# Indexer scores of two heads in one insertion between the projection units of a two-layer decoder

## The chip, the cores and the metric

The kernel runs on one core of a Trainium2 chip. The metric is the device time in microseconds of one execution, from the first to the last instruction; lower is better. Five engines work side by side, each through its own list of instructions in order: TensorE (PE, with its weight loads shown apart as PEld), VectorE (DVE), ScalarE (ACT), GpSimd (POOL) and SyncE (SP, which here only issues loads). They meet in semaphores.

## The reference, cut to what matters

Two decoder layers on 256 tokens of width 2048. A layer has one combined projection, three token mixers (sparse attention, a convolution, cross-attention into 256 memory tokens), a gated merge, and an MLP. The part that the change touches is the indexer of the sparse attention:

```python
# 16 indexer heads of width 64; iq (tokens, 16, 64), ik (tokens, 64), iw (tokens, 16)
s_idx = jnp.einsum('bqhd,bsd->bqhs', iqb, ik).astype(jnp.float32)
index = jnp.einsum('bqh,bqhs->bqs', iwb.astype(jnp.float32), jax.nn.relu(s_idx)) * idx_scale
causal = key_pos[None, :] <= q_pos[:, None]
index = jnp.where(causal[None], index, -jnp.inf)
sel_val, sel_idx = lax.top_k(index, topk)      # topk = 64 of 256 keys
```

Tokens are handled in two tiles of 128. A query of the first tile may only see keys 0 to 127, so its scores with keys 128 to 255 are masked whatever they are.

## The kernel before, in words

Nearly all the work is projection. Each 512-column block of a weight matrix is a group of 8 units; a unit (L535 to L548) holds 256 rows of the matrix. SP loads the weights in chunks of 1 MB, two units each. ACT copies a unit to a rounded high part `hi` (L805), DVE subtracts to get the low part `lo` (L1075), and PE multiplies: 12 matmuls of 128x128 by 512 columns (L545 to L547), accumulated in one of two PSUM buffers. `hi` and `lo` have four slots, so ACT may fill unit n once PE has finished unit n - 4, and PE can be up to four units behind what DVE delivers.

Everything else is written into this stream by hand. A front of 11 groups (88 units, n = 0 to 87) and the first 32 units of the merge are unrolled, and a function `side(n)` on each engine says what follows unit n there. ACT, DVE and POOL do at unit n + 4 what belongs to PE's insertion after unit n (`EMPTY_AFTER = 4`). All waits are semaphores; no planner is involved.

The indexer scores are such insertions. After unit n = 36 + s, for s = 0 to 15, PE computes head s (`scores`, L598 to L601): for each of the two query tiles one float32 matmul of 64 rows against all 256 keys, into bank `s % 2` of the PSUM tile `sc`. The trace shows each float32 matmul as two weight loads and two matmuls, so a head has four of each. Even heads lie in partitions 0 to 63 of `iqT` and `ikT`, odd heads in 64 to 127 (`ik_twice` holds the keys twice). At its step 40 + s ACT takes the ReLU of the bank (L913, 128x512), and at the same step DVE adds it to `index` with the head's weight, one instruction for each query tile (L1216, L1218). At its step 55 POOL masks the 256 keys of both tiles (L1531).

Around this lie: fills (L558: four transposes of 128 columns) after units 38 to 41, 45 and 46; from DVE step 51 one convolution tap per step, from step 56 two or three (L1136), from step 58 on every third step a round of the top-k search (L1149, L1154); at ACT's step 52 and DVE's and POOL's step 53 the norm of the memory keys (L929, L931, L1257, L1518 to L1523). From n = 79 on the attention heads are inserted, with full 128-row score matmuls through the same line 601.

DVE works through its list in order. What it does for the index at a step stands ahead of the split of the next unit.

Of the kernel before, what the change touches and what calls it, by code (L numbers as in the profile page):

```python
# [93 lines left out]
INDEX_AT = 36  # L94
# [38 lines left out]
def fills_until(name):  # L133
# [24 lines left out]
              "tp_hi": 78, "score": 28, "sc0": 15, "sc1": 14, "squared": 24, "x_new": 20,  # L158
              "dve_step": 153, "pool_step": 106, "gain_in": 48, "mem_in": 32, "front_in": 16 * FRONT_DMAS,
              "ln_in": 32, "bias_in": 32 * CB, "parked": 32, "x_back": 16, "mean_ready": 3, "rstd_ready": 3,  # L160
              "scaled": 10, "ik_here": 2, "ikwT_here": 1, "ik_turned": 1, "iq_turned": 2,
              "relu_used": IDX_HEADS, "causal_done": 2, "chosen": 1,
# [65 lines left out]
def build(nc, x, mem, positions, norm1_g, w_in, q_norm_g, k_norm_g, mem_norm_g, w_mem_kv, mq_norm_g,  # L228
# [3 lines left out]
    with ctx:  # L232
# [4 lines left out]
        def at(name, shape, offset, dt=F32):  # L237
            n = 4
            for s in shape[1:]:
                n *= s  # L240
            assert base + offset + n <= nc.sbuf_usable_end, name
            return nc.alloc_sbuf_tensor_at(name, shape, dt, offset=base + int(offset))
# [50 lines left out]
        relu = at("relu", [P, 2, T, SEQ], S + 22 * kb)  # L293
        index = at("index", [P, T, SEQ], S + 26 * kb)
# [64 lines left out]
        sc = ctx.enter_context(nc.psum_tensor("sc", [P, 2, T, SEQ], F32))  # L359

# [166 lines left out]
        def _(pe):  # L527
# [70 lines left out]
            def scores(bank, pairs):  # L598
                pe.wait_ge(sc_free[bank], here.next(f"sc{bank}"))
                for t, (a, b) in enumerate(pairs):  # L600
                    mm = pe.matmul(sc[:, bank, t, :], a, b, start=(t == 0), stop=(t == T - 1),  # L601
                                   skip_group_check=True)
                mm.then_inc(sc_full, 1)

            def head_output(j):

                emptied(("p", j, 0))
                b = here.fill(("o", j, 0))
                pe.wait_ge(tp_free[b], here.now(f"tp{b}"))
                o = tp[:, b, 0:2, :].rearrange("p a d -> p (a d)")  # L610
                for kt in range(T):
                    if j < MEM_HEADS:
                        v = mv_tok[:, kt, j]
                    else:
                        v = kv_tok[:, kt, KV_HEADS + (j - MEM_HEADS) // (HEADS // KV_HEADS)]
                    pT = mem_pT if j < MEM_HEADS else attn_pT
                    mm = pe.matmul(o, v, pT[:, j % 2, kt, :], start=(kt == 0), stop=(kt == T - 1))  # L617
                mm.then_inc(tp_full, 1)

            def side(n):  # L620
# [55 lines left out]
                if INDEX_AT <= n < INDEX_AT + IDX_HEADS:  # L676
                    j, a = divmod(n - INDEX_AT, 2)
                    if n == INDEX_AT:
                        emptied(("ik", 0, 0), ("iq", 1, 1))
                    half = slice(a * IDX_DIM, (a + 1) * IDX_DIM)  # L680
                    scores(a, [(iqT[half, j, t * P:(t + 1) * P], ikT[half, :]) for t in range(T)])
# [108 lines left out]
        def _(act):  # L790
# [50 lines left out]
            def side(n):  # L841
# [66 lines left out]
                s = n - INDEX_AT - EMPTY_AFTER  # L908
                if s in range(IDX_HEADS):
                    act.wait_ge(sc_full, here.next("score"))  # L910
                    if s >= 2:
                        act.wait_ge(relu_used, here.next("relu_used"))
                    act.activation(relu[:, s % 2], sc[:, s % 2], ACT.Relu).then_inc(sc_free[s % 2], 1)  # L913
                    if s == IDX_HEADS - 1:
                        here.next("relu_used", 2)
# [137 lines left out]
        def _(dve):  # L1053
# [123 lines left out]
            def side(n):  # L1177
# [28 lines left out]
                if n - INDEX_AT - EMPTY_AFTER in range(IDX_HEADS):  # L1206
                    s = n - INDEX_AT - EMPTY_AFTER
                    if s == 0:
                        here.next("sc0")
                        dve.wait_ge(ik_turned, here.next("ik_turned"))  # L1210
                    here.next(f"sc{s % 2}")
                    dve.wait_ge(sc_free[s % 2], here.now(f"sc{s % 2}") + 1)
                    for t in range(T):
                        w = iw[:, t, s:s + 1]
                        if s == 0:
                            ins = dve.tensor_scalar(index[:, t], relu[:, 0, t], w, None, ALU.mult)  # L1216
                        else:
                            ins = dve.scalar_tensor_tensor(index[:, t], relu[:, s % 2, t], w, index[:, t],  # L1218
                                                           ALU.mult, ALU.add)
                    ins.then_inc(relu_used, 1)  # L1220
                    dve.wait_ge(relu_used, here.next("relu_used"))
                    here.next("score")
# [220 lines left out]
        def _(pool):  # L1443
# [30 lines left out]
            def side(n, l):  # L1474
# [53 lines left out]
                if n == INDEX_AT + EMPTY_AFTER + IDX_HEADS - 1:  # L1528
                    pool.wait_ge(relu_used, here.next("relu_used", IDX_HEADS))
                    alone()  # L1530
                    pool.affine_select(out=index[:, :, :], in_=index[:, :, :], pattern=[[P, T], [-1, SEQ]],  # L1531
                                       compare_op=ALU.is_ge, fill=UNSEEN, base=0,
                                       channel_multiplier=1).then_inc(causal_done, 1)
# [128 lines left out]
```

## Time and profile before

| | us |
|---|---|
| median of 3 executions (lowest, highest) | 2988.55 (2987.88, 2988.84) |
| profiled execution, its span (no other time of it is given) | 2989.6 |
| PE busy | 2917.6 (98%) |
| PE weight loads busy | 2389.9 (80%) |
| DVE busy | 1748.7 (58%) |
| ACT busy | 1355.1 (45%) |
| POOL busy | 318.0 (11%) |
| DMA, mean | 187 GB/s |
| indexer score matmuls, 128 in the trace | 402 ns each on average |

The span counts from the first to the last instruction of the profiled execution, 1.05 us more than the median, which is under 0.04%. Matmuls are pipelined: the next starts while the last one's result drains, so the distance between two starts is what a matmul costs, and the busy time of one is longer. In the timeline a row is: start, duration, engine, line, operation, output and inputs, rows*columns of the array, shapes, and how many instructions were merged into it; brackets hold the idle time before it and what ended it. For each layer the indexer scores lie in one stretch, about 115 to 180 us and 1599 to 1664 us from the span's start.

### The profile page before, as it was taken

How to read it: one execution, taken by the hardware profiler on the slowest of the kernel's cores; microseconds unless marked ns; L12 is line 12 of the kernel's file. 1: busy time of each engine (PE TensorE's matmuls, PEld its weight loads, DVE VectorE, ACT ScalarE, POOL GpSimd, SP SyncE). 2: the span in 40 equal slices, each digit the busy share in tenths (PEclk: the TensorE clock that was granted, in tenths of full speed). 3: DMA queues.
4: the chain of work that ended last, by engine and by line, in shares of the span. 5: the costliest groups of instructions: out<-in, count | busy, mean ns of one | idle time of the engine just before them, and what ended most of it. 6: DMA issues, size and time to landing. Idle time of an engine off the chain costs nothing.

```text
span 2989.6 us, 38386 instructions
## 1 busy us (share of the span) xinstructions
PE 2917.6 (98%) x13120; PEld 2389.9 (80%) x13120; DVE 1748.7 (58%) x1849; ACT 1355.1 (45%) x1673; POOL 318.0 (11%) x329
## 2 busy tenths in 40 slices
PE   7998899999999999999999989999999999999998
PEld 6776788888888888888877767888888888888887
DVE  4689655556555555555545896555565545555554
ACT  5443654444443444434445436444444434344443
POOL 1158300000000000000020682000000000000000
PEclk9999999999999999999999999999999999999999
DMA  7544456565655656555564444666556565565653
GB/s 270 187 162 131 151 170 210 192 228 197 203 185 191 191 188 188 189 188 190 186 220 169 149 141 145 183 208 225 197 200 202 188 190 190 186 192 185 196 184 127
DMA packets 274090, 558.65 MB, mean 187 GB/s; under 512 B 13168, under 2 KB 13168, under 8 KB 271376
## 3 DMA queue, kind: packets, MB, share of 16 engines
q1 hardware_dynamic: 266384, 523.53, 53.1%
q0 software_dynamic: 5888, 30.02, 3.4%
q10 hardware_dynamic: 1664, 3.15, 0.3%
q8 instruction: 84, 1.38, 0.2%
q14 instruction: 70, 0.57, 0.1%
HBM read 550.37 MB, written 6.29 MB: 186 GB/s over the span
## 4 chain that ended last, share of the span: by engine, by line
PE 88%; DVE 6%; issue 4%; ACT 1%; DMA 1%; DVEq 0%; POOL 0%; ACTq 0%; POOLq 0%
PE acc L545 28%; PE acc L547 28%; PE acc L546 28%; DVE conv_acc L1136 3%; PE tp L558 3%; PE sc L601 1%; DVE lo L1075 1%; ACT hi L805 1%; PE tp L617 1%; DMA conv_bias<-in_conv_o_b 1%; DVE index L1154 0%; DVE index L1218 0%; DMA pos_i<-in_positions 0%; DVE head_sum L1257 0%; DVE s_buf L1166 0%
## 5 line engine op out<-in xcount | busy, mean ns | idle before, releaser
L1075 DVE TENSOR_TENSOR lo<-raw,hi 128x1024 fp32r<-128x1024 f32 (+1 forms) x1008 | 1237.6, 1230 | 1191.9 <-ACT hi L805 1182.9
L805 ACT ACTIVATE hi<-raw 128x1024 fp32r<-128x1024 f32 (+1 forms) x1008 | 1055.7, 1048 | 1489.4 <-PE acc L547 1485.3
L545 PE MATMUL acc<-hi,hT_hi 128*128 128x512 f32 x2304 | 924.7, 401 | 34.5 <-DVE lo L1075 34.4
L547 PE MATMUL acc<-hi,hT_lo 128*128 128x512 f32 x2304 | 903.6, 392 | 0.0
L546 PE MATMUL acc<-lo,hT_hi 128*128 128x512 f32 x2304 | 902.9, 392 | 0.0
L545 PE MATMUL acc<-hi,bT_hi 128*128 128x512 f32 x1408 | 556.4, 395 | 0.0
L547 PE MATMUL acc<-hi,bT_lo 128*128 128x512 f32 x1408 | 548.8, 390 | 0.0
L546 PE MATMUL acc<-lo,bT_hi 128*128 128x512 f32 x1408 | 548.5, 390 | 0.0
L545 PEld LDWEIGHTS acc<-hi,hT_hi 128*128 128x128 f32 x2304 | 436.0, 189 | 133.2 <-DVE lo L1075 44.6
L547 PEld LDWEIGHTS acc<-hi,hT_lo 128*128 128x128 f32 x2304 | 435.6, 189 | 93.9
L546 PEld LDWEIGHTS acc<-lo,hT_hi 128*128 128x128 f32 x2304 | 436.7, 190 | 87.0
L545 PEld LDWEIGHTS acc<-hi,bT_hi 128*128 128x128 f32 x1408 | 264.4, 188 | 64.2 <-issue 11.7
L547 PEld LDWEIGHTS acc<-hi,bT_lo 128*128 128x128 f32 x1408 | 264.3, 188 | 55.8
L546 PEld LDWEIGHTS acc<-lo,bT_hi 128*128 128x128 f32 x1408 | 264.6, 188 | 52.7
L1136 DVE SCALAR_TENSOR_TENSOR conv_acc<-uT,tapT,conv_acc 128x256 f32<-128x256 f32 x180 | 115.2, 684 | 0.5
L1605 POOL DMA_DIRECT2D x_park<-x_tok x4 | 2.2, 546 | 750.6 <-ACT sc L823 750.6
L1555 POOL TENSOR_SCALAR tap_part<-uT,tapT 128x256 f32<-128x256 f32 x60 | 75.6, 1260 | 10.4 <-POOL conv_acc L1557 9.9
L1557 POOL TENSOR_TENSOR conv_acc<-conv_acc,tap_part 128x256 f32<-128x256 f32 x60 | 65.7, 1094 | 11.7 <-POOL tap_part L1555 11.7
L1346 DVE TENSOR_TENSOR x_tok<-acc,x_tok 128x1024 f32<-128x1024 f32 x40 | 48.7, 1218 | 16.9 <-PE acc L547 16.9
L1576 POOL DMA_DIRECT2D gate_bias<-in_gate_b x8 | 6.3, 791 | 487.9 <-DVE merged L1328 471.8
L955 ACT ACTIVATE s_buf<-s_buf,p_inv 128x256 f32<-128x256 f32 x48 | 21.8, 501 | 73.5 <-DVE p_inv L1269 73.2
L1083 DVE TENSOR_TENSOR bT_lo<-tp,bT_hi 128x512 fp32r<-128x512 f32 x80 | 54.6, 683 | 0.0
(223 smaller groups left out, 1689.1 us busy)
## 6 DMA issues: line engine op xcount, KB each, us to landing
raw<-in_w_in SPq DMA_DIRECT2D x160, 1024.0 KB, 5.0
raw<-in_w_up SPq DMA_DIRECT2D x128, 1024.0 KB, 5.2
raw<-in_w_down SPq DMA_DIRECT2D x128, 1024.0 KB, 5.1
raw<-in_w_out SPq DMA_DIRECT2D x32, 1024.0 KB, 5.1
raw<-in_w_mem_kv SPq DMA_DIRECT2D x16, 1024.0 KB, 5.1
raw<-in_w_attn_o SPq DMA_DIRECT2D x16, 1024.0 KB, 5.1
raw<-in_w_conv_o SPq DMA_DIRECT2D x8, 1024.0 KB, 5.1
raw<-in_w_mem_o SPq DMA_DIRECT2D x8, 1024.0 KB, 5.1
```

The source lines that it names most:

```text
L545: pe.matmul(o, a1, w1, start=first and dk == 0, stop=False)
L546: pe.matmul(o, a1, w2, start=False, stop=False)
L547: mm = pe.matmul(o, a2, w1, start=False, stop=last and dk == 1)
L558: mm = pe.transpose(tp[0:m, b, i, 0:k], tile, ident[0:k, 0:k])
L601: mm = pe.matmul(sc[:, bank, t, :], a, b, start=(t == 0), stop=(t == T - 1), skip_group_check=True)
L805: act.activation(hi[:, u % 4, :, 0:w], raw[:, c, 2 * (u % 2):2 * (u % 2) + 2, 0:w], ACT.Copy).then_inc(hi_ready, 1)
L1075: dve.tensor_tensor(lo[:, u % 4, :, 0:w], raw[:, u // 2, 2 * (u % 2):2 * (u % 2) + 2, 0:w], hi[:, u % 4, :, 0:w].bitcast(F32), ALU.subtrac ...
L1083: ins = dve.tensor_tensor(dst, tp[:, b, 0:n, :], src.bitcast(F32), ALU.subtract)
L1136: step(dve.scalar_tensor_tensor(conv_acc[:, c], src, tapT[:, c, k:k + 1], conv_acc[:, c], ALU.mult, ALU.add))
L1346: dve.tensor_tensor(xb, acc[:, pair], xb, ALU.add).then_inc(x_new, 1)
L1555: link(pool.tensor_scalar(tap_part[:, :], uT[:, c, k:k + SEQ], tapT[:, c, k:k + 1], None, ALU.mult))
L1557: ins = pool.tensor_tensor(conv_acc[:, c], conv_acc[:, c], tap_part[:, :], ALU.add)
```

## The change

Two heads share an insertion. `index_pair(j)` stands after units 36, 38, ... 50 and computes heads 2j and 2j + 1: the second query tile first, against 256 keys, the even head on array rows 0 to 63 and then the odd head on rows 64 to 127; then the first query tile in the same order, against keys 0 to 127 only. Each head has a PSUM bank of its own. ACT takes one ReLU of 128x768 and then frees both banks; DVE has four instructions for each pair, two of 256 and two of 128 columns, each waiting for the one before the last; POOL fills the unused quarter of `index` with a constant and masks only the two diagonal 128x128 blocks, one step earlier. The buffer `relu` grows from 4 to 6 KB of a partition, and `index` moves behind it.

```diff
--- before.py
+++ after.py
@@ -91,7 +91,9 @@
 IKW_FILL = [20, 21]
 IK_FILL = 28
 IQ_FILL = [[16, 17], [31, 32]]
-INDEX_AT = 36
+INDEX_PAIR_AT = [36 + 2 * j for j in range(IDX_HEADS // 2)]
+SEEN = [slice(SEQ, SEQ + P), slice(0, SEQ)]
+SEEN_KEYS = SEQ + P
 CONV_IN_FILL = [45, 46]
 MK_FILL = [57, 58]
 MQ_FILL = [73, 74]
@@ -155,11 +157,11 @@
 
 PER = {
     "layer": {"group": GROUPS, "unit": GROUPS * UNITS, "acc0": 35, "acc1": 35, "fill": 112, "tp0": 56, "tp1": 56,
-              "tp_hi": 78, "score": 28, "sc0": 15, "sc1": 14, "squared": 24, "x_new": 20,
-              "dve_step": 153, "pool_step": 106, "gain_in": 48, "mem_in": 32, "front_in": 16 * FRONT_DMAS,
+              "tp_hi": 78, "score": 20, "sc0": 15, "sc1": 14, "squared": 24, "x_new": 20,
+              "dve_step": 177, "pool_step": 107, "gain_in": 48, "mem_in": 32, "front_in": 16 * FRONT_DMAS,
               "ln_in": 32, "bias_in": 32 * CB, "parked": 32, "x_back": 16, "mean_ready": 3, "rstd_ready": 3,
               "scaled": 10, "ik_here": 2, "ikwT_here": 1, "ik_turned": 1, "iq_turned": 2,
-              "relu_used": IDX_HEADS, "causal_done": 2, "chosen": 1,
+              "relu_ready": IDX_HEADS // 2, "relu_used": IDX_HEADS // 2, "causal_done": 2, "chosen": 1,
               "glu_here": 1, "glu_tanh": 1, "glu_done": 1, "pad_ready": 1, "conv_done": 1,
               "conv_start": 1, "conv_rest": 1, "ln_stat": 1,
               "ln_root": 1, "ln_done": 1, "ln_scaled": 1, "y_tanh_ready": 1, "swish_done": 1, "rows_here": 5,
@@ -290,8 +292,8 @@
         oT_lo = at("oT_lo", [P, HEADS, SEQ], S + 38 * kb, F32R)
         moT_hi = at("moT_hi", [P, MEM_HEADS, SEQ], S + 46 * kb, F32R)
         moT_lo = at("moT_lo", [P, MEM_HEADS, SEQ], S + 50 * kb, F32R)
-        relu = at("relu", [P, 2, T, SEQ], S + 22 * kb)
-        index = at("index", [P, T, SEQ], S + 26 * kb)
+        relu = at("relu", [P, 2, 2, SEEN_KEYS], S + 22 * kb)
+        index = at("index", [P, T, SEQ], S + 28 * kb)
         hidden = at("hidden", [P, 2, T, COL], S + 22 * kb)
         glu_a = at("glu_a", [P, T, CONV], S + 30 * kb)
         glu_g = at("glu_g", [P, T, CONV], S + 34 * kb)
@@ -357,6 +359,7 @@
         acc = ctx.enter_context(nc.psum_tensor("acc", [P, 2, T, COL], F32))
         tp = ctx.enter_context(nc.psum_tensor("tp", [P, 2, 4, P], F32))
         sc = ctx.enter_context(nc.psum_tensor("sc", [P, 2, T, SEQ], F32))
+        sc_seen = sc[:, :, :, :].rearrange("p a t s -> p a (t s)")
 
         x_park = nc.dram_tensor("x_park", (T, P, D), F32, kind="Internal").ap()
 
@@ -602,6 +605,17 @@
                                    skip_group_check=True)
                 mm.then_inc(sc_full, 1)
 
+            def index_pair(j):
+
+                for a in range(2):
+                    pe.wait_ge(sc_free[a], here.next(f"sc{a}"))
+                for t in (1, 0):
+                    for a in range(2):
+                        half = slice(a * IDX_DIM, (a + 1) * IDX_DIM)
+                        mm = pe.matmul(sc_seen[:, a, SEEN[t]], iqT[half, j, t * P:(t + 1) * P], ikT[half, 0:(t + 1) * P],
+                                       start=(t == 1), stop=(t == 0), skip_group_check=True)
+                mm.then_inc(sc_full, 1)
+
             def head_output(j):
 
                 emptied(("p", j, 0))
@@ -673,12 +687,11 @@
                         fill(name, [s_buf[:, i % 3, t, k * P:(k + 1) * P] for k in range(T) for t in range(T)])
                     elif what == "o":
                         head_output(i)
-                if INDEX_AT <= n < INDEX_AT + IDX_HEADS:
-                    j, a = divmod(n - INDEX_AT, 2)
-                    if n == INDEX_AT:
+                if n in INDEX_PAIR_AT:
+                    j = INDEX_PAIR_AT.index(n)
+                    if j == 0:
                         emptied(("ik", 0, 0), ("iq", 1, 1))
-                    half = slice(a * IDX_DIM, (a + 1) * IDX_DIM)
-                    scores(a, [(iqT[half, j, t * P:(t + 1) * P], ikT[half, :]) for t in range(T)])
+                    index_pair(j)
                 if n in HEAD_AT:
                     j = HEAD_AT.index(n)
                     h = j - MEM_HEADS
@@ -905,13 +918,16 @@
                     here.next("scaled")
                     for b in range(CB):
                         square_sum(wide[:, b * COL:(b + 1) * COL], mem_sum[:, t, b:b + 1])
-                s = n - INDEX_AT - EMPTY_AFTER
-                if s in range(IDX_HEADS):
+                if n - EMPTY_AFTER in INDEX_PAIR_AT:
+                    j = INDEX_PAIR_AT.index(n - EMPTY_AFTER)
                     act.wait_ge(sc_full, here.next("score"))
-                    if s >= 2:
+                    if j >= 2:
                         act.wait_ge(relu_used, here.next("relu_used"))
-                    act.activation(relu[:, s % 2], sc[:, s % 2], ACT.Relu).then_inc(sc_free[s % 2], 1)
-                    if s == IDX_HEADS - 1:
+                    act.activation(relu[:, j % 2], sc_seen[:, :, 0:SEEN_KEYS], ACT.Relu).then_inc(relu_ready, 1)
+                    act.wait_ge(relu_ready, here.next("relu_ready"))
+                    for a in range(2):
+                        act.sem_inc(sc_free[a], 1)
+                    if j == len(INDEX_PAIR_AT) - 1:
                         here.next("relu_used", 2)
                 if n == GLU_TANH:
                     act.wait_ge(glu_here, here.next("glu_here"))
@@ -1203,21 +1219,26 @@
                     dve.tensor_tensor(wide[:, :], wide[:, :], gain[:, :], ALU.mult).then_inc(scaled, 1)
                 if n == MEM_MEAN:
                     means(1, mem_sum)
-                if n - INDEX_AT - EMPTY_AFTER in range(IDX_HEADS):
-                    s = n - INDEX_AT - EMPTY_AFTER
-                    if s == 0:
+                if n - EMPTY_AFTER in INDEX_PAIR_AT:
+                    j = INDEX_PAIR_AT.index(n - EMPTY_AFTER)
+                    if j == 0:
                         here.next("sc0")
                         dve.wait_ge(ik_turned, here.next("ik_turned"))
-                    here.next(f"sc{s % 2}")
-                    dve.wait_ge(sc_free[s % 2], here.now(f"sc{s % 2}") + 1)
-                    for t in range(T):
-                        w = iw[:, t, s:s + 1]
-                        if s == 0:
-                            ins = dve.tensor_scalar(index[:, t], relu[:, 0, t], w, None, ALU.mult)
-                        else:
-                            ins = dve.scalar_tensor_tensor(index[:, t], relu[:, s % 2, t], w, index[:, t],
-                                                           ALU.mult, ALU.add)
-                    ins.then_inc(relu_used, 1)
+                    dve.wait_ge(relu_ready, here.next("relu_ready"))
+                    for a in range(2):
+                        here.next(f"sc{a}")
+                        for t in range(T):
+                            w, seen, keys = iw[:, t, 2 * j + a:2 * j + a + 1], relu[:, j % 2, a, SEEN[t]], (t + 1) * P
+                            if j == a == 0:
+                                step(dve.tensor_scalar(index[:, t, 0:keys], seen, w, None, ALU.mult))
+                            else:
+                                settle(1)
+                                ins = dve.scalar_tensor_tensor(index[:, t, 0:keys], seen, w, index[:, t, 0:keys],
+                                                               ALU.mult, ALU.add)
+                                if a == 1 and t == T - 1:
+                                    ins.then_inc(relu_used, 1)
+                                else:
+                                    step(ins)
                     dve.wait_ge(relu_used, here.next("relu_used"))
                     here.next("score")
                 if n == GLU_A_TAKEN:
@@ -1525,10 +1546,12 @@
                         link(ins)
                         ins = rotate(dest, HALF_A, 0)
                     ins.then_inc(rows_ready, 1)
-                if n == INDEX_AT + EMPTY_AFTER + IDX_HEADS - 1:
-                    pool.wait_ge(relu_used, here.next("relu_used", IDX_HEADS))
+                if n == INDEX_PAIR_AT[-1] + EMPTY_AFTER:
+                    pool.wait_ge(relu_used, here.next("relu_used", IDX_HEADS // 2))
                     alone()
-                    pool.affine_select(out=index[:, :, :], in_=index[:, :, :], pattern=[[P, T], [-1, SEQ]],
+                    link(pool.memset(index[:, 0, P:SEQ], UNSEEN))
+                    diagonal = index[:, :, :].rearrange("p t (k s) -> p (t k) s", s=P)[:, 0:4:3, :]
+                    pool.affine_select(out=diagonal, in_=diagonal, pattern=[[0, T], [-1, P]],
                                        compare_op=ALU.is_ge, fill=UNSEEN, base=0,
                                        channel_multiplier=1).then_inc(causal_done, 1)
                 if n == TOPK_AT + 3 * (TOPK // 8 - 1) + 1:
```

## Rows read from the trace of the kernel before

**Rows 1.** The page: busy times, and the chain that ended last.
```profile
PE 2917.6 (98%) x13120; PEld 2389.9 (80%) x13120; DVE 1748.7 (58%) x1849; ACT 1355.1 (45%) x1673; POOL 318.0 (11%) x329
...
PE 88%; DVE 6%; issue 4%; ACT 1%; DMA 1%; DVEq 0%; POOL 0%; ACTq 0%; POOLq 0%
```

**Rows 2.** Busy us by stretch: PE, PEld, DVE, ACT, POOL, clock, DMA share, GB/s.
```profile
112.00:182.00 70.00, 70.00 (x296) 51.21 (x295) 45.97 (x68) 33.64 (x44) 6.75 (x4) 1.00 0.41 135
182.00:325.00 143.00, 125.47 (x537) 99.25 (x536) 129.59 (x201) 63.49 (x94) 107.42 (x90) 0.96 0.46 150
```

**Rows 3.** Timeline of PE, one insertion and the next unit.
```profile
115.31 0.39 PE L547 MATMUL acc<-hi,hT_lo 128*128 128x512 f32 x1
115.63 1.13 PE L601 MATMUL sc<-ikT,iqT 64*128 64x256 f32 x4
...
117.26 0.39 PE L547 MATMUL acc<-hi,hT_lo 128*128 128x512 f32 x1
...
119.31 0.39 PE L547 MATMUL acc<-hi,hT_lo 128*128 128x512 f32 x1
119.63 1.13 PE L601 MATMUL sc<-ikT,iqT 64*128 64x256 f32 x4
```

**Rows 4.** The indexer score matmuls of the stretch from 112 to 182 us.
```profile
L601 PE MATMUL sc<-ikT,iqT x64: 375/376/481, 115.6 to 179.1; 64*128 64x256 f32 x64
```

**Rows 5.** Timeline of PE, a fill and a head in one insertion.
```profile
123.31 0.39 PE L547 MATMUL acc<-hi,hT_lo 128*128 128x512 f32 x1
...
124.07 1.13 PE L601 MATMUL sc<-ikT,iqT 64*128 64x256 f32 x4
...
125.70 0.39 PE L547 MATMUL acc<-hi,hT_lo 128*128 128x512 f32 x1
```

**Rows 6.** Timeline of PE, scores of an attention head, full 128 rows.
```profile
343.10 0.39 PE L547 MATMUL acc<-hi,hT_lo 128*128 128x512 f32 x1
343.33 1.02 PE L601 MATMUL sc<-kT,qT 128*128 128x256 f32 x4
...
344.66 0.40 PE L547 MATMUL acc<-hi,hT_lo 128*128 128x512 f32 x1
```

**Rows 7.** Instructions on `index`: count, least/median/most ns, first and last start.
```profile
L1218 DVE SCALAR_TENSOR_TENSOR index<-relu,iw,index x60: 471/479/2620, 122.0 to 1667.7; 128x256 f32<-128x256 f32 x60
L1149 DVE MAX8 top<-index x32: 276/344/408, 192.6 to 1748.3; 128x8 f32<-128x128 f32 x16, 128x8 f32<-128x256 f32 x16
```

**Rows 8.** Timeline of ACT, a unit's split and a ReLU.
```profile
119.73 1.06 ACT L805 ACTIVATE hi<-raw 128x1024 fp32r<-128x1024 f32 x1 [2.34 <-PE acc L547]
120.79 0.60 ACT L913 ACTIVATE relu<-sc 128x512 f32<-128x512 f32 x1
```

**Rows 9.** Timeline of DVE, steps 54 to 56 of layer 1.
```profile
175.52 1.23 DVE L1075 TENSOR_TENSOR lo<-raw,hi 128x1024 fp32r<-128x1024 f32 x1
176.67 0.87 DVE L1218 SCALAR_TENSOR_TENSOR index<-relu,iw,index 128x256 f32<-128x256 f32 x2
...
181.33 3.02 DVE L1218 SCALAR_TENSOR_TENSOR index<-relu,iw,index 128x256 f32<-128x256 f32 x2
...
184.87 1.65 DVE L1075 TENSOR_TENSOR lo<-raw,hi 128x1024 fp32r<-128x1024 f32 x1
```

**Rows 10.** Timeline of POOL beside them.
```profile
180.50 3.16 POOL L1523 TENSOR_TENSOR mk_tok<-mk_tok,head_gain 128x1024 f32<-128x1024 f32 x1 [0.18 <-POOL mk_tok L1520]
184.59 0.85 POOL L1531 TENSOR_SCALAR_AFFINE_SELECT index<-index 128x512 f32<-128x512 f32 x1 [0.93 <-DVE index L1218]
```

**Rows 11.** The chain that ended last, from the insertion after unit 50.
```profile
174.40 1.06 PE sc L601 x4
...
178.43 1.07 ACT hi L805
```

**Rows 12.** Timeline of PE, where it first waits after the scores.
```profile
229.77 0.50 PE L545 MATMUL acc<-hi,hT_hi 128*128 128x512 f32 x1 [0.17 <-DVE lo L1075]
```

**Rows 13.** Timeline of DVE, the same place in layer 2.
```profile
1665.20 3.01 DVE L1218 SCALAR_TENSOR_TENSOR index<-relu,iw,index 128x256 f32<-128x256 f32 x2
```

## The prediction

> **What bounds the kernel now.** I read the page's shares first. PE is busy for 2917.6 of 2989.6 us, and 88% of the chain that ended last lies on it [rows 1]. That share is a mean over the whole program, so the second view is the busy time by stretch. In the indexer stretch of layer 1, 112 to 182 us, PE is busy for 70.00 of 70 us while DVE has 45.97 and ACT 33.64, at a clock share of 1.00, the 2.4 GHz level. In the stretch behind it, 182 to 325 us, PE has 125.47 of 143 us and DVE 129.59 [rows 2]. So there are two regimes: during the scores every nanosecond taken from PE comes off the end of the stretch; afterwards DVE sets the pace.
>
> The third view is PE's timeline, read by starts. Unit matmuls follow each other at (119.31 - 117.26) / 9 = 0.228 us. From the last of one unit (115.31) to the third of the next (117.26) lie 1.95 us with a head between them; without it they would be three distances, 0.68 us. A head costs 1.27 us, and the period from one head to the next, 4.00 us, says the same: 12 x 0.228 + 1.27 [rows 3]. With a fill in the same insertion the step is 2.39 us [rows 5], so 1.71 for both. The same four passes on 128 rows (343.10 to 344.66) cost 1.56 - 0.68 = 0.88 us [rows 6]. The difference, 0.39 us, is what entering and leaving the 64-row form costs. Within the insertion, four passes run from first start to last end in 1.13 us, the last one lasting 0.376 [rows 3, 4]; its start is thus 0.75 us behind the first. Four passes of 0.216 us (0.864) fill the 0.88 us of the 128-row case and the 1.27 less 0.39 of this one.
>
> The Trainium skill (TensorEngine Tiling (Array Packing), Key Properties) says that a change of tiling mode drains TensorE, while another tile of the same mode does not. The 0.39 us agree with the first half. For the second half no row stands, since no insertion uses both halves; it would leave one 0.39 for each pair, as in my sum.
>
> **The change, part by part.** PE before: 16 heads a layer, 1.27 us each where they stand alone. With the fill that shares six of the insertions, 1.71 less the 0.44 of a fill (four passes of 128 columns at half of 0.216) is again 1.27. That is 20.3 us a layer.
>
> PE after: 8 pairs, each one drain of 0.39 there and back. The second tile has four passes of 256 columns (two heads, two passes), 4 x 0.216 = 0.86; the first tile four of 128 columns, 4 x 0.108 = 0.43. Strictly one after another that is 1.30, and a pair costs 1.69 us. If both halves of the array worked side by side all the time, it would be half, 0.65, and a pair 1.04 us. No row shows two halves at work at once. The two passes of one head share their rows and follow at the full 0.216 [rows 3, 4], so they cannot overlap. The second pass of the even head and the first of the odd one have other rows, other weights and another PSUM bank. In program order that gives 0.216 (even, first), 0.216 (even second with odd first), 0.216 (odd second with the first pass of the next tile's even head), then 0.108, and 0.108 for the last: 0.86. I take it, between the bounds: a pair costs 0.39 + 0.86 = 1.25, say 1.27 us, the same as one head now. The nearest row, passes of one half at 0.216 each, would give 1.69 instead, and that is the first rival.
>
> The Trainium skill (TensorE: Matmul & The Clock Gate, Part 3: Packing small matmuls) holds that matmuls on different row groups run at once, with starts about 4 ns apart, in program order. That speaks for the overlap and is shown nowhere in this trace; by it the pair is at 0.87 us of passes, by the rows of one half at 1.30.
>
> How the gain reaches the end. The DVE-bound stretch begins at the last heads. The chain runs on PE until unit 51 ends, 178.43, then over ACT's copy into DVE [rows 11]. DVE adds the last head in 3.02 us instead of 0.87, because one of the two instructions takes 2.62 us [rows 7, 9]; POOL's 3.16 us multiplication of `mk_tok` lies over it [rows 10]. It begins the split of step 56 at 184.87. Unit 50 ended at 174.40, so this is 10.47 us behind [rows 9, 11]. In layer 2 the same 3.01 us stand [rows 13].
>
> Ahead of the end of unit 50 lie 14 heads before and 7 pairs after: 14 x 1.27 - 7 x 1.27 = 8.9 us earlier. From there, after: pair 1.27, units 51 and 52 2 x 2.73, ACT's copy 1.06 [rows 8] give 7.8 us until step 56 can start, if DVE is free. DVE's index work of the last pair is at step 54: four instructions at 0.39 apart for 256 columns (0.87 for two) and about 0.26 for 128 (the top-k maximum loses 0.13 us for 128 columns less: 0.408 to 0.276 [rows 7]), 1.3 to 1.8 us with the waits. Step 55 has none. POOL's long multiplication follows DVE's norm step and comes at about the same distance from unit 50, +6.1 to +9.3 us. It may hold a convolution tap or the split of step 55 as it now holds the index, so step 56 starts between +7.8 and +9.5. The hand-over gains 1.0 to 2.7 us; I take 1.5, nearer to the held case. A layer gains 8.9 + 1.5 = 10.4, both 20.8 us.
>
> From step 56 on DVE does the same work as before, from an earlier start. PE waits first at 229.77 [rows 12], and its waits come from DVE's splits, so they move with it. So do the fills, the bias load that POOL issues behind them, and the weight loads: those run at 135 GB/s in this stretch and at 150 in the next [rows 2], and a stretch shortened by a seventh asks for about 155.
>
> What costs nothing, and what covers it. ACT's ReLU grows from 512 to 768 columns: 0.60 for 512 and 1.06 for 1024 [rows 8] give about 0.83 us. It takes the place of two of 0.60, and ACT idles 2.34 us ahead of a split. Both banks come free about 1 us after the insertion and are wanted 5.4 us later. DVE now waits for the ReLU with the next split queued behind it, and PE waits for that split only when four units are used up: 10.9 us, against some 2.5 for insertion and ReLU plus 1.8 of index work. A pair's period on DVE, two splits, four index instructions and two taps, is about 2.5 + 1.8 + 1.0 = 5.3 us; on PE it is 2 x 2.73 + 1.27 = 6.7. Without the cover each microsecond of DVE above 6.7 would cost seven times a layer. POOL has one more instruction and a smaller mask, one step earlier; before, the mask ended at 185.4 [rows 10] and top-k asked for it at 192.6 [rows 7]. Buffer sizes and addresses move no work.
>
> The sum is made against the profiled execution, whose span is 2989.6; the median is 1.05 us less. I subtract from the median: 2988.55 - 20.8 = 2967.8. The clock may give or take: a piece at the 1.2 GHz level falls in the DVE-bound stretch (its clock share is 0.96 [rows 2]), and its place can shift against PE's waits by a microsecond or two. I round to **2968**.
>
> **The rivals.** *The halves take turns.* Passes follow each other as they do in one half: a pair costs 1.69, a layer gains 17.8 - 11.8 + 1.5 = 7.5, both 15.0, time 2973.6. For it: nothing in the trace overlaps but a load with a matmul. Against it: the two halves share neither rows nor bank.
>
> *Each change of half drains once.* Three changes within a pair at 0.20, half of the 0.39: a pair 2.28, a layer gains 17.8 - 16.0 + 1.5 = 3.3, time 2982. Against it: both are of the same 64-row form.
>
> *Each change of half costs a whole 0.39.* This ends on the other side: a pair costs 1.69 + 3 x 0.39 = 2.86 us, seven of them 20.0 against 17.8, minus 1.5: slower by 0.7 a layer, and without the hand-over's gain by 2.2, both 4.4: time 2990 to 2993. It decides from 17.8 / 7 = 2.54 us a pair. For it: a full price is what one visit costs now. Against it: the 0.39 pays for two changes.
>
> *DVE keeps its end.* If something other than PE's progress starts the DVE-bound stretch, PE only waits longer in it: time 2988. For it: PE waits 17 of the 143 us [rows 2]. Against it: the chain hands over from a unit's end [rows 11].
>
> **How the numbers follow.** Chances: overlap as forecast, full or in part, 0.52; turns 0.30; one drain each 0.08; whole price each 0.03; DVE keeps its end 0.07. With both halves always busy and the whole hand-over gain (2.7) a layer gains 17.8 - 7.3 + 2.7 = 13.2, time 2962; turns with a hand-over gain of nothing give 2977, and the clock's microsecond or two lies on top. The range 2963 to 2979 leaves out the last three cases, 0.18. About 6 us, 0.2%, is what a measurement can tell from no change. Faster: 0.52 + 0.30 and half of the third, 0.86; within 0.2%: 0.12, the other half and DVE's case, with a little of the fourth; slower 0.02.
>
> **What would show it.** PE's timeline: two units, then one insertion of eight passes; from the last unit matmul to the third of the next 1.95 us if the halves overlap, 2.37 if they take turns, near 3 with drains. Starts of the odd head's first pass right at the even one's second: overlap. DVE's split of step 56 8 to 9.5 us behind the end of unit 50. PE's waits of the DVE-bound stretch no longer than before, and begun earlier. The forecast is wrong if PE waits inside the scores, if the insertion costs over 1.7, or if the gain at unit 56 is gone by 420 us.

## The result, and the profile after

| | before | after |
|---|---|---|
| median (lowest, highest), 4 executions each | 2988.7 (2987.88, 2989.8) | 2965.95 (2965.34, 2967.76) |
| span of the profiled execution | 2989.6 | 2966.1 |
| PE busy | 2917.6 | 2891.1 |

The change takes off 22.7 us: ratio 0.9925, 95% interval 0.9912 to 0.9938. Two further comparisons of the same two kernels gave 0.9936 (0.9923 to 0.995; medians 2967.99 against 2988.01) and 0.993 (0.9917 to 0.9944; 2967.49 against 2988.32). So 20 to 23 us are gained; 2968 was forecast, and the range of 2963 to 2979 holds all three medians. One execution of one variant below (all keys for the first tile) lasted 8961 us, three times as long as any other, and stands in no number here.

PE's timeline around one insertion answers to [rows 3]:

```profile
116.21 0.39 PE L550 MATMUL acc<-hi,hT_lo 128*128 128x512 f32 x1
116.53 0.92 PE L615 MATMUL sc<-ikT,iqT 64*128 64x256 f32 x8
117.38 0.50 PE L548 MATMUL acc<-hi,hT_hi 128*128 128x512 f32 x1
...
117.95 0.40 PE L550 MATMUL acc<-hi,hT_lo 128*128 128x512 f32 x1
```

Eight passes end 0.92 us after the first begins, where four took 1.13. From 116.21 to 117.95 is 1.74 us; less three distances that is 1.06 (1.061 in all ten insertions without a fill), against 1.27 for one head before. The same view cut off at 116.6 us merges only what has started by then:

```profile
116.53 0.49 PE L615 MATMUL sc<-ikT,iqT 64*128 64x256 f32 x2
```

Two passes begin together, and 0.49 is one pass (0.48) and hardly more. All eight run in pairs, and the two of a pair start 0.006 us apart: 2 x 0.216 + 2 x 0.108 = 0.65.

The busy times by stretch answer to [rows 2] (same columns; the stretches are moved with their work):

```profile
112.00:169.00 57.00, 57.00 (x290) 45.18 (x289) 40.97 (x66) 29.25 (x37) 2.42 (x2) 1.00 0.49 158
169.00:314.00 145.00, 125.35 (x549) 98.83 (x548) 132.99 (x204) 64.87 (x95) 108.28 (x92) 0.99 0.45 147
```

PE is still without a gap in the first, and in the second DVE is busy for 132.99 of 145 us. The entry of that stretch answers to [rows 9]; below it is POOL's timeline, to [rows 10]:

```profile
167.16 1.23 DVE L1091 TENSOR_TENSOR lo<-raw,hi 128x1024 fp32r<-128x1024 f32 x1
168.30 1.40 DVE L1236 SCALAR_TENSOR_TENSOR index<-relu,iw,index 128x128 f32<-128x128 f32 x4
169.74 0.49 DVE L1152 SCALAR_TENSOR_TENSOR conv_acc<-uT,tapT,conv_acc 128x256 f32<-128x256 f32 x1
170.14 2.92 DVE L1091 TENSOR_TENSOR lo<-raw,hi 128x1024 fp32r<-128x1024 f32 x1
172.98 2.61 DVE L1152 SCALAR_TENSOR_TENSOR conv_acc<-uT,tapT,conv_acc 128x256 f32<-128x256 f32 x1
175.52 1.21 DVE L1091 TENSOR_TENSOR lo<-raw,hi 128x1024 fp32r<-128x1024 f32 x1
```

```profile
170.07 1.92 POOL L1541 TENSOR_TENSOR mk_tok<-mk_tok,head_rstd 128x1024 f32<-128x1024 f32 x1 [0.18 <-POOL head_rstd L1539]
172.16 3.15 POOL L1544 TENSOR_TENSOR mk_tok<-mk_tok,head_gain 128x1024 f32<-128x1024 f32 x1 [0.18 <-POOL mk_tok L1541]
```

The index work of the last pair, 1.40 us from 168.30, is now clear of POOL's two multiplications. But the split of step 55 takes 2.92 us and the tap behind it 2.61. So the split of step 56 (175.52) starts 10.39 us behind the end of unit 50, where it was 10.47 before.

The starts of the same unit's first matmul in both traces say where the time went (after minus before, us):

| unit | 36 | 51 | 56 to 64 | 72 | 88 | 92 | 100 | 104 | 119 |
|---|---|---|---|---|---|---|---|---|---|
| layer 1 | +0.90 | -9.47 | -10.72 | -9.50 | -9.70 | -11.29 | -11.28 | -11.02 | -11.03 |
| layer 2 | -11.66 | -22.03 | -23.28 | -22.01 | -21.97 | -21.98 | -21.97 | -23.70 | -23.70 |

In each layer PE alone gains 11.6 us by unit 56, counted from unit 36. Between 64 and 72, where PE begins to wait for DVE, 1.2 us are given back: 10.4 stay. Then come two steps of 1.6 and 1.7 us, at units 88 to 92 of layer 1 and 100 to 104 of layer 2. Both lie at a piece at the 1.2 GHz level, a few us in which PE's granted clock falls to the lower of its two levels. In the first stretch the trace of before has two such pieces and the one of after has one; in the second it is one against none. Twice 10.4 and the two steps, less the 0.9 of a later start, make 23.2; the spans lie 23.5 apart.

### The profile page after: what moved, and what is told of

It is laid out like the page before. It is cut to its first block, busy times and chain, and to the rows that moved or that the text cites. A ratio compares the mean times of both kernels' runs of the same rounds, so it can differ in the third digit from the quotient of the medians.

```text
span 2966.1 us, 38416 instructions
## 1 busy us (share of the span) xinstructions
PE 2891.1 (97%) x13120; PEld 2376.0 (80%) x13120; DVE 1745.2 (59%) x1849; ACT 1347.8 (45%) x1657; POOL 313.6 (11%) x331
## 4 chain that ended last, share of the span: by engine, by line
PE 88%; DVE 5%; issue 4%; DMA 1%; ACT 1%; DVEq 0%; ACTq 0%; POOL 0%; POOLq 0%; SPq 0%
PE acc L548 28%; PE acc L550 28%; PE acc L549 28%; DVE conv_acc L1152 3%; PE tp L561 3%; DVE lo L1091 1%; ACT hi L818 1%; PE tp L631 1%; DMA conv_bias<-in_conv_o_b 1%; PE sc L615 0%; PE sc L604 0%; DVE index L1170 0%; DMA x_tok<-in_x 0%; DMA raw<-in_w_in 0%; DVE head_sum L1278 0%
```

## The experiments

Each was timed in 5 rounds against the kernel before, beside the profile. Positions in the stretch are from the profile and repeat to 0.01 us. The times scatter by some us; the clock pieces, below, are one cause that the traces show.

**Which half takes what.** Three variants of the pair, and one part alone.

*Same rows for both heads:*

```diff
-                        half = slice(a * IDX_DIM, (a + 1) * IDX_DIM)
+                        half = slice(0, IDX_DIM)
```

> The kernel after the change, but both heads of a pair read the lower 64 rows (the odd head's product is computed from the even head's data; same count, shapes and banks). It takes the overlap away and keeps everything else. If the overlap of the halves is what made the insertion 1.06 us, the eight passes follow one another: 4 x 0.216 + 4 x 0.108 = 1.30 plus 0.39 for entering and leaving: 1.70 us, 16 x 0.64 = 10.2 us more: 2976. If the passes are short for another reason (two banks, fewer keys), 1.06 us and 2966 stay.

Measured: 2976.81 us (2975.84 to 2980.63), ratio 0.9959 (0.9947 to 0.9972). The insertion costs 1.705 us. The view cut off at 116.9 us shows one pass where the changed kernel had two:

```profile
116.85 0.48 PE L615 MATMUL sc<-ikT,iqT 64*128 64x256 f32 x1
```

The passes take turns, as the first rival had it, when they share rows. Each head has its own bank here too, so two banks do not bring the overlap about; different rows do. The 0.64 us between 1.705 and 1.061 are the whole worth of the second half of the array. Whether the overlap would survive with both heads in one bank was not tried.

*Head by head instead of alternating:*

```diff
-                for t in (1, 0):
-                    for a in range(2):
+                for a in range(2):
+                    for t in (1, 0):
```

> The kernel after the change with the two loops of the pair exchanged: both query tiles of the even head, then both of the odd one, so the four matmul instructions are in the order lower, lower, upper, upper rows instead of alternating. If each half of the array takes its instructions on its own as soon as they are in the queue, nothing changes: insertion 1.06 us, time 2966. If matmuls start in the order in which they are written and only neighbours on different rows overlap, only the boundary overlaps: passes 0.216 + 0.216 + 0.108, then the even head's last beside the odd head's first, then 0.216 + 0.108 + 0.108: about 1.08 us of passes, insertion 1.48, 16 x 0.42 = 6.7 us more: 2972.6. If the halves took turns in both kernels, no change.

Measured: 2968.18 us (2967.35 to 2970.71), ratio 0.9929 (0.9916 to 0.9941). The insertion costs 1.067 us:

```profile
115.77 0.93 PE L615 MATMUL sc<-ikT,iqT 64*128 64x256 f32 x8
```

PE's positions are within 0.1 us of the changed kernel's up to unit 88 of both layers. The cut at 115.8 us shows two passes already begun, though the odd head's stands behind all of the even head's in the program:

```profile
115.77 0.49 PE L615 MATMUL sc<-ikT,iqT 64*128 64x256 f32 x2
```

All four passes of 256 columns start within 0.34 us, ahead of the first of 128 columns at 0.54, although the even head's 128 columns are written ahead of the odd head's 256. So each half takes its instructions on its own, and alternating them is not needed for the overlap. The Trainium skill (TensorE: Matmul & The Clock Gate, Part 3: Packing small matmuls) has concurrent row groups, which this shows for float32. It also says that matmuls start and end strictly in program order; the starts of this trace disagree across the two halves, and the measurement decides.

*All keys for the first tile again:*

```diff
-                        mm = pe.matmul(sc_seen[:, a, SEEN[t]], iqT[half, j, t * P:(t + 1) * P], ikT[half, 0:(t + 1) * P],
+                        mm = pe.matmul(sc_seen[:, a, (1 - t) * SEQ:(2 - t) * SEQ], iqT[half, j, t * P:(t + 1) * P], ikT[half, :],
```

> The kernel after the change, but the first query tile is again multiplied with all 256 keys (the surplus 128 columns are computed and not read); everything else, ReLU and index included, stays at half the keys for that tile. It isolates what halving the keys gives PE once two heads share an insertion. If the two halves of the array work side by side throughout, an insertion is 4 passes of 0.216 us in pairs: from the last unit matmul to the third of the next, less three distances, 1.27 us instead of 1.06, and 16 x 0.21 = 3.4 us more in all: 2969.3. If PE's time behind the scores is set by DVE anyway (rival), the time stays at 2966. If only neighbouring passes of the two heads overlapped (my forecast before), the insertion would be 0.39 + 5 x 0.216 = 1.47 us.

Measured: 2974.78 us (2970.15 to 2975.61), ratio 0.9946 (0.9933 to 0.9958). The insertion costs 1.274 us, as expected:

```profile
115.99 1.13 PE L615 MATMUL sc<-ikT,iqT 64*128 64x256 f32 x8
```

Relative to the changed kernel's unit 36, PE is 1.54 us a layer later at unit 56 and 1.3 at unit 72. That explains 2.6 to 3.1 us and not the 7.0 between the two spans. The rest are three steps of 1.6 us (units 88 to 92 in both layers, 100 to 104 in layer 2), each with a piece at 1.2 GHz that the other trace lacks. The time missed the expectation; the mechanism did not.

*One head for each insertion, half the keys* (in full with ReLU, index and mask as in the change):

```diff
-                    scores(a, [(iqT[half, j, t * P:(t + 1) * P], ikT[half, :]) for t in range(T)])
+                    pe.wait_ge(sc_free[a], here.next(f"sc{a}"))
+                    for t in (1, 0):
+                        mm = pe.matmul(sc_seen[:, a, SEEN[t]], iqT[half, j, t * P:(t + 1) * P],
+                                       ikT[half, 0:(t + 1) * P], start=(t == 1), stop=(t == 0),
+                                       skip_group_check=True)
+                    mm.then_inc(sc_full, 1)
```

> The kernel before the change with one part of it alone: one head for each insertion as before (16 of them), but only 128 keys for the first query tile, in matmul, ReLU, index and mask. An insertion should be 0.39 + 2 x 0.216 + 2 x 0.108 = 1.05 us against 1.27: 32 x 0.22 = 7.0 us less than before: 2981.7, and 2980 to 2984 with the start of the DVE-bound stretch. If the entry cost of the 64-row form depends on the work in it, or if DVE's side sets the gain, it would be under 2 or over 10 us. With the loss of full_keys against the changed kernel it tells how the total of 22.7 us is made up: halving first 7.0, then pairing 15.7.

Measured: 2982.95 us (2982.41 to 2983.69), ratio 0.9977 (0.9968 to 0.9987): 7.7 us off before's 2990.61 on that chip, 7.0 expected. One head costs 1.054 us. That is the price of a pair in the changed kernel: the second head is free there. Of the gain, halving alone gives 6 to 8 us (3.0 a layer at unit 72, 7.7 in the medians), and pairing the rest. In the other order, with the pairs already there, halving was worth only 1.3 us a layer at unit 72 (full_keys).

**Why the hand-over gave nothing.** Two kernels leave out POOL's two multiplications of the memory keys, all but one column of 128: one is the changed kernel without them, the other the kernel before:

```diff
-                    link(pool.tensor_tensor(dest, dest, over(head_rstd[:, 0:T * heads].rearrange(
-                        "p (t h) -> p t h", t=T), 3, HEAD), ALU.mult))
...
-                    ins = pool.tensor_tensor(dest, dest, g, ALU.mult)
+                    if k == 0:
+                        ins = pool.tensor_tensor(dest[:, :, :, 0:1], dest[:, :, :, 0:1],
+                                                 over(head_rstd[:, 0:T * heads].rearrange(
+                                                     "p (t h) -> p t h", t=T), 3, 1), ALU.mult)
...
```

> The changed kernel without POOL's two multiplications of the memory keys with their norm and their gain (left out of the computation but for one column), 1.9 and 3.2 us long, which lie over DVE's steps 54 and 55. Theory: they hold up DVE's instructions (2.92 for a split of 1.23, 2.61 for a tap of 0.48: 3.8 us), and so step 56 starts 10.4 us behind the end of unit 50 though its input is there after 7.6. Without them: step 56 at +7.6 to +8, 2.4 us a layer earlier, 4.8 in all: 2961. Rival: those durations are DVE's own, or what follows needs the same time from POOL: no change, 2966.

Measured: 2963.49 us (2962.18 to 2967.6), ratio 0.9926 (0.9912 to 0.9939). DVE's steps 55 and 56:

```profile
170.49 1.22 DVE L1091 TENSOR_TENSOR lo<-raw,hi 128x1024 fp32r<-128x1024 f32 x1
171.64 0.63 DVE L1152 SCALAR_TENSOR_TENSOR conv_acc<-uT,tapT,conv_acc 128x256 f32<-128x256 f32 x1
173.16 1.28 DVE L1091 TENSOR_TENSOR lo<-raw,hi 128x1024 fp32r<-128x1024 f32 x1 [0.90 <-ACT hi L818]
```

The split is back to 1.22 us, the tap to 0.63, and step 56 waits for ACT. It starts 6.89 us behind the start of unit 51, against 9.61, and PE's unit 72 comes 2.17 us a layer earlier (2.4 expected). The median is 4.5 us below the changed kernel's on that chip, 2967.99, but above the 2961 expected.

> The kernel before the change, with the same two multiplications left out. There they held DVE for 3.2 us (1.88 for a split, 2.62 for an index instruction, 1.65 for a split). Without them step 56 should start when its input is there, 9.1 us behind the end of unit 50 instead of 10.5: 1.4 us a layer, 2.8 in all: 2986 to 2988. If so, the change would be worth 2.0 us more where POOL is quiet, which is the hand-over gain that I had forecast and did not get. Rival: nothing changes, or both kernels gain the same.

Measured: 2986.01 us (2983.29 to 2988.34), ratio 0.9996 (0.9987 to 1.0005), which the time alone cannot tell from no change. In the trace step 56 waits for ACT here too:

```profile
183.96 1.41 DVE L1075 TENSOR_TENSOR lo<-raw,hi 128x1024 fp32r<-128x1024 f32 x1 [1.38 <-ACT hi L805]
```

It starts 8.14 us behind the start of unit 51 instead of 9.49, and unit 72 comes 1.06 us a layer earlier (1.4 expected). One of the three durations that the expectation counts was not the multiplications' work: the 1.65 us of a split begins at 184.87, 1.2 us after they ended. So POOL costs the changed kernel about 1 us a layer more than it cost the one before. The medians point the same way: 22.5 us between these two kernels, 20.0 between the two whole ones on that chip. The timelines fit an exchange of waits: DVE's split of step 55 (170.14) gets through only after POOL's first multiplication (until 171.99), POOL's second, begun at 172.16, after the split (173.06), and the tap, begun at 172.98, after that (175.31). The kernel before had the same exchange, with the last index instructions in the tap's place:

```profile
178.43 1.90 POOL L1520 TENSOR_TENSOR mk_tok<-mk_tok,head_rstd 128x1024 f32<-128x1024 f32 x1 [0.18 <-POOL head_rstd L1518]
179.52 1.88 DVE L1075 TENSOR_TENSOR lo<-raw,hi 128x1024 fp32r<-128x1024 f32 x1 [1.38 <-ACT hi L805]
```

There the split began 1.09 us after POOL's first multiplication, and from that one's end (180.33) it took 1.07 us. Now it begins 0.07 us after it, and again ends 1.07 us behind its end. The split comes at a worse moment and lasts 1.04 us longer, which is of the size of the 1 us a layer. The Trainium skill (SBUF — State Buffer, SBUF: two separate sides) says this: the two engines share a pair of ports under an exclusive lock held for a whole instruction, and DVE takes part with two inputs from SBUF. The trace agrees, 2.92 us against 1.22.

**Looking for a better version.** Two tries to move convolution taps from DVE's bound stretch into the one that PE bounds.

```diff
-DVE_CONV = [(51, 1), (52, 1), (53, 1), (54, 1), (55, 1)] + [(n, 2 + n % 2) for n in range(56, 92)]
+DVE_CONV = [(n, 2) for n in range(51, 67)] + [(n, 2 + n % 2) for n in range(67, 92)]
```

> The changed kernel with five convolution taps of a layer moved on DVE from steps 57 to 65 (two instead of three at the odd ones) to steps 51 to 55 (two instead of one), into the stretch that PE bounds. Same work. Theory: DVE bounds from step 56 on, so five taps of about 0.5 us less there move its end 2.5 us earlier, less up to 0.9 that the added taps of steps 54 and 55 cost: 1.6 to 2.5 us a layer, 3 to 5 in all: 2961 to 2963. Rival: DVE has no room left in steps 51 to 55 after the change, or PE waits just as long for something later (heads, the bias load): 2966.

Measured: 2966.3 us (2963.53 to 2968.76), ratio 0.9932 (0.9918 to 0.9945); 2961 to 2963 was expected, and the changed kernel has 2967.99 on that chip. Unit 72 came only 0.43 us a layer earlier: the split of step 55 lasted 3.46 us, and step 56 started 11.06 us behind unit 51 instead of 9.61. Second try, with the taps ahead of POOL's multiplications:

```diff
+DVE_CONV = [(51, 3), (52, 3), (53, 1), (54, 1), (55, 1)] + [(n, 2) for n in range(56, 64)] + [(n, 2 + n % 2) for n in range(64, 92)]
```

> The changed kernel with four convolution taps of a layer moved on DVE from steps 57, 59, 61 and 63 to steps 51 and 52 (three each instead of one). In the first try the added taps of steps 54 and 55 met POOL's multiplications and step 56 started 1.45 us later. Steps 51 and 52 lie ahead of these and DVE idles 1.2 and 1.6 us behind them. Theory: step 56 starts 9.6 us behind the start of unit 51 as in the changed kernel, and PE's unit 72 comes 4 x 0.5 = 2.0 us a layer earlier, less what shifted meetings with POOL cost (0.65 in the first try): 1.3 to 2.0 us a layer, 2.6 to 4.0 in all, 2962 to 2965 where the changed kernel has 2966 to 2968. Rival: POOL's own chain of taps is pushed into the place that DVE leaves, so the time of a step in 57 to 65 stays and the gain is under 0.5 us a layer.

Measured: 2968.05 us (2966.1 to 2968.84), ratio 0.9931 (0.9917 to 0.9944). Its mechanism held: step 56 started 9.68 us behind unit 51, and unit 72 came 1.4 us a layer earlier than in the changed kernel beside it. The time did not follow. The 2.7 us went in steps of 1.5 and 1.6 us at pieces of the 1.2 GHz level (units 100 to 104 of layer 1, 88 to 92 of layer 2). The busy times by stretch, of this kernel and then of the changed one, 1770 to 1900 us (the clock is the third number from the end):

```profile
1770.00:1900.00 130.00, 123.92 (x567) 102.53 (x568) 80.17 (x102) 72.60 (x128) 20.65 (x16) 0.97 0.53 161
```

```profile
1770.00:1900.00 130.00, 123.04 (x570) 101.92 (x571) 81.02 (x102) 73.72 (x132) 20.46 (x16) 0.99 0.54 162
```

The mean clock of its five executions is 0.994 to 0.995, against 0.995 to 0.996. Neither try is clear of the changed kernel.

**The changed kernel again**, twice, as partner on the chips of these runs.

> The changed kernel once more, unaltered, beside the runs below on their chip, for the pieces of its execution at the 1.2 GHz level. In its first profile there were 2 such pieces in layer 1 and 1 in layer 2 (beside those at the start of a layer and the end), against 4 and 2 before the change; each one missing is worth half of its 3.41 us, 1.7. If this is a property of the kernel, the new profile shows 3 again and the time is 2966; if it is a matter of where the pieces fall in one execution, the count differs, and the time moves by 1.7 us for each.

Measured: 2967.99 us (2964.92 to 2970.49). From unit 36 to unit 88 of each layer PE's distances are those of the first profile to 0.05 us. But it has two pieces at 1.2 GHz in layer 1 and four in layer 2, and from unit 88 on it gains 1.95 us once and loses 1.6 twice against the first profile (two of the four, at units 86 to 88 where PE waits for DVE anyway, leave its positions as they were). In the stretch from 1745 to 1825 us, which holds all four, the clock is 0.91; in the first profile, with one there, 0.98:

```profile
1745.00:1825.00 80.00, 67.71 (x288) 54.27 (x289) 53.53 (x70) 45.05 (x87) 35.92 (x29) 0.91 0.45 139
```

```profile
1745.00:1825.00 80.00, 65.90 (x299) 52.63 (x299) 54.88 (x74) 43.48 (x84) 38.61 (x32) 0.98 0.47 144
```

So steps of this size come and go between two executions of one kernel. That the two in the comparison of spans are such chance too, and not the change, is inferred from this; only one execution of each timing was profiled.

> The changed kernel once more, as the partner of the run above on its chip; no change is expected: 2966 to 2968, unit 72 where it was.

Measured: 2967.49 us (2966.34 to 2967.64), as expected.

## Why the prediction was right

**PE bounds the scores, and what it saves comes off.** Right. Units 36 to 56 lost 11.6 us in each layer, with PE busy throughout.

**The price of an insertion: 1.27 us forecast, 1.06 measured.** The mechanism was right, the term mis-sized: 0.86 us of passes where there are 0.65. The step that failed is the order: I took all passes to stand in one list and only neighbours on different rows to overlap, so that the even head's first pass ran alone. It ran beside the odd head's first, as if each half had a list of its own (head_by_head), and the lower bound, 0.65, was the true value; I had it at 1.04 us a pair. The sign on record for overlap was 1.95 us from the last unit matmul to the third of the next; it came out at 1.74. The entry and exit, 0.39 us for each insertion, came out right in four kernels: 1.705, 1.274, 1.061 and 1.054 less 1.30, 0.86, 0.65 and 0.65 leave 0.40 to 0.41. The rivals with turns or more drains are refuted.

**The count ahead of the hand-over.** 14 heads less 7 pairs at 1.06 us are 10.3 us a layer where I had 8.9, and the difference is the price of a pair. In the traces unit 50 ends 10.2 us earlier, counted from unit 36.

**The hand-over: 1.5 us a layer forecast, 0.1 measured.** Wrong within its reasoning. Step 56 started 10.39 us behind the end of unit 50 instead of 10.47; my bracket went from +7.8 to +9.5. The step that failed: I kept POOL's multiplications at the same distance from unit 50 and let them hold one instruction, the tap or the split. They held both, as they had held both the split of step 55 (1.88 us) and the index before, and the split longer than before; the second multiplication ran from +7.0 to +10.2 us instead of +6.1 to +9.3. The gain at the hand-over is there when POOL is quiet in both kernels: step 56 then starts 7.67 us behind the end of unit 50 instead of 9.13. POOL takes it back, with 2.7 us in the changed kernel against 1.35 in the one before.

**The sum.** The two errors, +1.3 and -1.4 us a layer by the positions, cancel: 10.4 forecast; 10.2 up to unit 50, 0.1 at the hand-over, 10.4 measured at unit 72 and 20.8 in all. That the total agrees so closely is luck. The comparisons of medians, 22.7, 20.0 and 20.8, lie around it. The 2.0 us by which the first measured median is below 2968 is of the size of one piece at 1.2 GHz; that this is what set that median is argued from the spans, not shown for each execution.

**What costs nothing.** Right: the ReLU of 768 columns takes 0.797 us (0.83 expected), the four index instructions 1.40 (1.3 to 1.8 expected), PE never waits inside the scores, and the longer mask, 1.31 us instead of 0.85 although it covers half the columns, lies ahead of the top-k search. **DVE keeps its end** is refuted by the 10.4 us at unit 72; its grain of truth is the 1.2 us that PE gained and DVE did not pass on, about the worth of the 16th head, which lay inside DVE's stretch already. Most of it came back as one new wait of PE for DVE, 0.83 us at unit 68 of each layer; before, PE first waited at unit 70. The sign on record, waits no longer than before, did not hold to that extent.

## What to carry to other kernels

Where a matmul needs 64 rows, put two independent ones on the two halves: the second was free, and their order did not matter. Here each had its own bank; one bank for both was not tried. Gather such work: each visit to the 64-row form cost 0.4 us between full-array matmuls, so 16 visits less save some 6 us before any overlap (an estimate, 16 x 0.39). A gain ahead of a stretch bound by another engine is to be counted up to the step where that stretch begins, and there against what the third engine does to it; read positions of the same instruction in both traces, since 2 to 3 us can hide in medians of runs whose clock pieces change.

## What the runs showed of the hardware that I had not expected

- The two row halves run float32 passes independently of program order: starts 0.006 us apart when alternated, 0.014 us apart when the odd head's matmuls stood last.
- A float32 pass costs 0.216 us for 256 columns and 0.108 for 128, on 64 or 128 rows alike, alone or beside one on the other half (the last ones of the kernel with the same rows for both heads came at 0.112).
- POOL's mask of two diagonal blocks, 256 columns a partition in a strided view, took 1.31 us, against 0.85 for 512 plain columns. Its place was ahead of POOL's own taps, and no other engine waited for it.
- Less waiting on PE did not mean less time: with taps_51_52 PE arrived 1.4 us a layer earlier and spent the gain at 1.2 GHz. Whether that is cause or coincidence, five executions at a mean clock of 0.994 to 0.995 suggest but do not show.
